# The second down product of a feed-forward, by rounded part for all token tiles first and by low part after

## The reference

```python
h2 = rms_norm(x, norm2_g[l])
x = x + (jax.nn.silu(h2 @ w_ffn_gate[l]) * (h2 @ w_ffn_up[l])) @ w_ffn_down[l]
```

## Time and profile before

| | |
|---|---|
| median of three runs | 2085.47 us |
| the profiled execution | 2088.51 us |
| its span, first to last instruction | 2086.5 us |
| TensorE, VectorE, GpSimd, ScalarE busy | 97%, 65%, 47%, 35% of the span |
| mean granted TensorE clock | 0.993 of full speed |
| one feed-forward chunk | 58.15 us |

### The profile page before, as it was taken

The page is one execution under the profiler, slowest core; times in us unless marked ns, Lnnn a source line. Parts: engine busy times, 40 slices in busy tenths (PEclk is TensorE's granted clock), DMA queues, the critical chain, the costliest instruction groups (busy, mean ns, idle before and its releaser), DMA issues. The chain is left out here.

```text
span 2086.5 us, 30135 instructions
## 1 busy us (share of the span) xinstructions
PE 2021.4 (97%) x9773; PEld 1644.7 (79%) x9773; DVE 1346.1 (65%) x2129; ACT 726.6 (35%) x1294; POOL 977.0 (47%) x827
## 2 busy tenths in 40 slices
PE   6999999999999999999999899997999999999998
PEld 5888888887777777777776788886888888888887
DVE  5768687753467667667657455468667656666666
ACT  4424333311334344334345200016343433333333
POOL 4413232322221122122121243348888889998987
PEclk9999999999999999999999999999999999999999
DMA  4112021223442442342454522210211111101112
GB/s 130 46 31 61 24 57 30 63 69 83 100 102 43 98 98 51 93 108 48 85 133 146 205 91 74 87 61 23 79 61 41 59 60 60 47 33 60 60 60 80
DMA packets 137744, 153.42 MB, mean 74 GB/s; under 512 B 7704, under 2 KB 112160, under 8 KB 137696
## 3 DMA queue, kind: packets, MB, share of 16 engines
q1 hardware_dynamic: 135952, 149.64, 26.1%
q10 hardware_dynamic: 1744, 3.15, 0.4%
HBM read 106.64 MB, written 20.97 MB: 61 GB/s over the span
## 5 line engine op out<-in xcount | busy, mean ns | idle before, releaser
L125 POOL TENSOR_TENSOR w_hi<-w_raw,w_ones 128x64 fp32r<-128x64 f32 x88 | 32.9, 374 | 1005.4 <-PE sb_g L151 463.4
L129 POOL TENSOR_TENSOR w_lo<-w_raw,w_hi 128x512 fp32r<-128x512 f32 x176 | 242.4, 1398 | 7.3
L813 DVE TENSOR_TENSOR sb_wt_lo<-sb_t,sb_wt_hi 128x512 fp32r<-128x512 f32 (+2 forms) x186 | 103.0, 554 | 113.1 <-ACT sb_wt_hi L634 111.3
L151 PE MATMUL sb_g<-h_hi,w_hi 128*128 128x512 f32 x544 | 152.8, 409 | 2.7 <-DVEq L693 1.9
L151 PE MATMUL sb_g<-h_lo,w_hi 128*128 128x512 f32 x544 | 150.5, 401 | 0.0
L151 PE MATMUL sb_g<-h_hi,w_lo 128*128 128x512 f32 x544 | 150.2, 400 | 0.0
L634 ACT CAST sb_wt_hi<-sb_t 128x512 fp32r<-128x512 f32 (+2 forms) x186 | 89.7, 482 | 166.5 <-PE sb_t L500 165.9
L151 PE MATMUL gla_g<-h_hi,w_hi 128*128 128x512 f32 x464 | 124.0, 402 | 0.0
L151 PE MATMUL gla_g<-h_lo,w_hi 128*128 128x512 f32 x464 | 122.8, 397 | 0.0
L151 PE MATMUL gla_g<-h_hi,w_lo 128*128 128x512 f32 x464 | 122.4, 397 | 0.0
L1844 DVE TENSOR_TENSOR y<-mp_out,y 128x512 f32<-128x512 f32 x104 | 70.7, 691 | 67.2 <-PE mp_out L1912 67.2
(11 more groups left out here) (500 smaller groups left out, 5161.5 us busy)
## 6 DMA issues: line engine op xcount, KB each, us to landing
w_raw<-w_in SPq DMA_DIRECT2D x64, 512.0 KB, 8.1
raw_g<-w_ffn_gate SPq DMA_DIRECT2D x11, 1024.0 KB, 5.2
ff_raw_u<-w_ffn_up SPq DMA_DIRECT2D x11, 1024.0 KB, 7.6
ff_raw_d<-w_ffn_down SPq DMA_DIRECT2D x11, 1024.0 KB, 4.8
sb_qs<-sb_q_st SPq DMA_DIRECT2D x32, 256.0 KB, 5.1
sb_kh<-sb_k_st SPq DMA_DIRECT2D x32, 256.0 KB, 5.0
sb_kl<-sb_k_st SPq DMA_DIRECT2D x32, 256.0 KB, 5.0
mp_sig<-gates_t SPq DMA_DIRECT2D x16, 512.0 KB, 4.2
```

The source lines that it names most:

```text
L125: self.nc.gpsimd.tensor_tensor(hi[:, 0:64], raw[:, 0:64], self.ones[:], ALU.mult)
L129: ins = self.nc.gpsimd.tensor_tensor(lo[:, at], raw[:, at], hi[:, at], ALU.subtract)
L151: ins = nc.tensor.matmul(acc, a[:, k, :], b[:, k, half * HALF:(half + 1) * HALF], start=(n == 0), stop=(n == len(steps) - 1))
L813: nc.vector.tensor_tensor(wt_lo[:, m % 2, a:HALF], weight_bank(m, last)[:, a:HALF], wt_hi[:, m % 2, a:HALF], ALU.subtract).then_inc(lo_rea ...
```

## The change

The second down product (P2) first runs hi by hi and hi by lo for the four token tiles, eight matmuls, and then lo by hi for the four, each of which counts its group in d_done. Ahead of the eight it waits for y_high of P2 in place of y_low of P2, and ahead of the last four for y_low. The matmuls of the other six products stay as they were, moved into a small function.

```diff
                 def down_block(ch):
                     for j, p in enumerate(D_ORDER):
                         pe.wait_ge(w_ready, d_first(ch) + j + 1)
-                        if p in (P1, P2, P6, P5):
-                            pe.wait_ge(y_low, 4 * ch + {P1: 1, P2: 2, P6: 3, P5: 4}[p])
+                        if p == P2:
+                            pe.wait_ge(y_high, 7 * ch + Y_HIGH[p])
+                        elif p in (P1, P6, P5):
+                            pe.wait_ge(y_low, 4 * ch + {P1: 1, P6: 3, P5: 4}[p])
                         else:
                             pe.wait_ge(y_low_pool, 3 * ch + {P7: 1, P3: 2, P4: 3}[p])
...
+                        passes = ((y_hi[p], hi), (y_hi[p], lo), (y_lo[p], hi))
+
+                        def multiply_group(g, first, last):
+                            for n in range(first, last):
+                                part, w = passes[n]
+                                ins = nc.tensor.matmul(D_CHAIN[p][g][:], part[:, g * P:(g + 1) * P], w,
+                                                       start=(start and n == 0), stop=(n == 2), skip_group_check=not start)
+                            return ins
+
+                        if p == P2:
+                            for g in range(NG):
+                                multiply_group(g, 0, 2)
+                            pe.wait_ge(y_low, 4 * ch + 2)
+                            for g in range(NG):
+                                multiply_group(g, 2, 3).then_inc(d_done, 1)
+                            continue
                         for g in range(NG):
-                            rows = slice(g * P, (g + 1) * P)
                             if j >= 2:
                                 pe.wait_ge(d_free, d_read(j - 2, g, ch))
-                            passes = ((y_hi[p], hi), (y_hi[p], lo), (y_lo[p], hi))
-                            for n, (part, w) in enumerate(passes):
-                                ins = nc.tensor.matmul(D_CHAIN[p][g][:], part[:, rows], w, start=(start and n == 0),
-                                                       stop=(n == 2), skip_group_check=not start)
-                            ins.then_inc(d_done, 1)
+                            multiply_group(g, 0, 3).then_inc(d_done, 1)
```

## The result

| | before | after |
|---|---|---|
| median of 17 runs each | 2087.66 us | 2091.41 us |
| the profiled execution | 2088.51 us | 2092.41 us |
| its span | 2086.5 us | 2090.4 us |
| one feed-forward chunk, mean of ten | 58.16 us | 58.54 us |

The changed kernel takes 1.0021 times as long, 95% interval 1.0014 to 1.0027: 4.4 us more, between 2.9 and 5.6 (the two medians themselves differ by 3.75). The forecast was 5.3 us more. The two executions differ by 0.7 us before the feed-forward chunks, the changed one being ahead. So times are compared by their distance from the start of the chunk's first down product, in the chunk shown 1537.34 before and 1537.04 after.

The account below looks back on a forecast made before the run. TensorE, busy 97%, was taken as the bound, its largest feed-forward wait before P2. Ten chunks at +0.61 - 0.17 = +0.44 give +4.4, the last +0.9: +5.3 on 2085.47 makes 2090.8 us, range 2081.5 to 2094.

Parts of the forecast that it names:

- P2 starts at once: Second down product: y_hi is ready in time, so it starts without waiting and ends 0.84 us earlier.
- 0.24 a matmul: Bound for P2's matmul spacing when visiting four PSUM tiles twice: 0.16 us a product; 0 was taken.
- VectorE's row then holds TensorE: Down products 2 and 3 wait for VectorE's adds to free PSUM tiles: product 2 by 0.27, product 3 starts 0.51 later.
- the signal: From the end of a recorded instruction to the start on the waiting engine: 0.12 us.
- late weight load: At product 3's start on TensorE: its weight load is not hidden after the wait, costing 0.10 us.
- the third rival: E product keeps its 0.17 and groups 1 to 3 of product 3 wait: +7.9 us, 2093.4 us; chance 12%.
- y_lo of P5 is held for 0.80 us: On VectorE: GpSimd's earlier y_lo of P7 makes it take 1.47 instead of 0.67, delaying every add behind it.
- The loss at E goes: First E product of gate and up: its w_lo is no longer last to come, winning 0.17 us a chunk.
- The last chunk: End of the feed-forward, set by VectorE's row of adds: y_lo of P5 ends later, costing 0.9 us.
- bound for slower: Whole run: a difference counts from 0.2%, 4.2 us, so slower means over 2089.6 us; chance of slower 0.54.
- VectorE wins the turn: Rival at y_lo of P5: GpSimd starts after VectorE, adds not delayed, -0.36 in ten chunks, 2081.9 us; chance 22%.
- The whole wait is won: Rival at P2's wait: 0.84 us won in ten chunks, -8.4 us, 2077.1 us; chance 6%.

Follow-up runs that it names:

- experiment 1: Changed kernel with VectorE's y_lo of P5 one place earlier, ahead of the fourth add of product 0: 2083.07 us, ratio 0.9984 to the kernel before.
- experiment 3: Changed kernel with one more wait, so GpSimd's y_lo of P7 starts only after VectorE's y_lo of P5: 2088.79 us, ratio 1.0009 to the kernel before.
- experiment 4: Changed kernel with one SBUF input of y_lo of P5 replaced by a PSUM tile (wrong number, timing only): 2082.74 us, ratio 0.9980 to the kernel before.
- experiment 7: Changed kernel with GpSimd's sum for P7 moved behind the lo part of the fifth down weights: 2076.61 us, ratio 0.9951 to the kernel before.
- experiment 6: Kernel before, with GpSimd's sum for P7 behind the fifth down weights' lo part and P4's weight sum ahead of y_lo of P7: 2084.13 us, ratio 0.9988.
- experiment 8: Changed kernel with GpSimd's weight sum for P4 moved ahead of y_lo of P7: 2082.89 us, ratio 0.9979 to the kernel before.
- experiment 5: Changed kernel, GpSimd's sum for P7 behind the fifth down weights' lo part, P4's weight sum ahead of y_lo of P7: 2076.6 us, ratio 0.9949 to kernel before.

## Why the prediction was right

The mechanism came out as forecast; two of its terms were mis-sized, in opposite directions, and that the sum still fits within 0.06 us a chunk is partly luck.

- **P2 starts at once.** As forecast: no wait, last matmul 5.21 after the chunk's first (forecast 5.22), nothing for visiting the tiles twice. Shown by the trace after. One bound was misread: the prediction gives 0.24 a matmul "as within P2 before", or 0.16 a product, but the ten matmul steps from 1541.10 to 1543.40 average 0.230, which is the 0.04 that it counts itself elsewhere.
- **VectorE's row then holds TensorE.** P6 0.21 late (forecast 0.27), product 3 at 9.43 (forecast 9.52). Most of the difference is the signal, the first term that was mis-sized: I took 0.12 us, as from y_lo to TensorE. From an add it is 0.05 to 0.06: the add of product 0's first tile ends at 1541.96 + 0.68 = 1542.64 and P6 starts at 1542.69; that of product 1 ends at 1546.41 and product 3 starts at 1546.47.
- **Product 3 is slower than forecast.** The second term: 0.10 was put down for its late weight load, and its 12 matmuls took 2.89 instead of 2.72, 0.17 more. The other 0.07 is of the kind that the third rival names (groups 1 to 3 lose a little); no experiment takes it apart. It offsets the shorter signal.
- **y_lo of P5 is held for 0.80 us.** Measured 1.46 instead of 0.67, 0.79 more; forecast 1.47. That this is the cause, and not a companion, experiments 1, 3 and 4 show, each by another handle: VectorE first, GpSimd later, one input in PSUM. In each y_lo takes 0.68 and product 3 starts 8.63 to 8.85 after the chunk's first product, not 9.43.
- **The loss at E goes.** 2.72 in every chunk instead of 2.83 to 2.92. Counted from the chunk's first product, w_lo of the first E product starts at 34.35 (1571.39 - 1537.04) instead of 34.82, and TensorE arrives later. Experiments 3 and 7 bring the loss back by moving GpSimd's row against TensorE's; experiment 6 takes it away in the kernel before.
- **The sum.** A chunk costs 0.38 more; forecast 0.44. The later start of product 3 is 0.42 and its own pace 0.17, against 0.17 won at E and 0.05 within product 5: 0.37. The last chunk costs 0.8 more from its first product to the last add; forecast 0.9. Ten times 0.38 and 0.8 are 4.6; the runs say 4.4. The forecast time of 2090.8 us lies nearer to the measured 2091.41 than the forecast difference to the measured one. That is luck: it was counted from the median of three runs, 2085.47, and that of 17 is 2087.66. The measured 4.4 also lies barely above the 4.2 that the prediction set as its bound for slower.
- **The rivals.** *VectorE wins the turn* did not happen in the changed kernel, but it describes well what happens once VectorE is not held: forecast 2081.9, that is 0.9983, and experiments 1, 4 and 8 measured 0.9984, 0.9980 and 0.9979. *The whole wait is won* needs VectorE's row freed, as experiment 5 shows: 0.9949, which holds besides the whole wait the loss at E and a shorter end.

What stays open: at what distance exactly a turn is won or lost. In the kernel before, one of VectorE's instructions for the hidden values (line 2447) lost the turn in three chunks, where it came 0.03 or 0.04 ahead of GpSimd's next instruction (1569.18 against 1569.21, and it took 1.87); in the other chunks it came 0.07 to 0.10 ahead and took 0.69. In experiments 5, 6 and 8, y_lo of P5 came 0.04 to 0.07 ahead in all eleven chunks and won each time. So the edge lies near 0.04 us, and the rows, which are given to 0.01, don't place it more closely. The changed kernel's case is clear of it: GpSimd was 0.38 ahead.

## What to carry to other kernels

When a wait on the bound engine goes, ask what its earlier end starts elsewhere, and whether two engines then meet that used to miss each other: here 0.84 us won started GpSimd early enough to hold one VectorE instruction for 0.8 us. Where VectorE and GpSimd both read two SBUF tiles, lay their rows side by side and put the one's waits where the other needs the turn; an instruction moved by one place was worth 7.7 us (1.0021 to 0.9984), and the original idea paid only once VectorE was no longer held.

## What the runs showed of the hardware

- A VectorE tensor_tensor with two SBUF inputs and a GpSimd tensor_tensor exclude each other for whole instructions, in both directions: VectorE 1.46 us instead of 0.68, GpSimd 1.62 to 1.78 instead of 1.29 (the trace after, experiments 1, 5 and 8). With one input in PSUM neither is held (experiment 4: 0.68 and 1.29).
- Of two such instructions that meet while GpSimd has one right behind the other, VectorE's lost the turn when it came 0.03 us ahead of GpSimd's next and took 1.87; it won when it came 0.07 ahead and took 0.68 (experiment 8).
- A signal from VectorE to TensorE took 0.12 us after y_lo and 0.05 to 0.06 us after an add, counted from the recorded end. I had not expected two values, and no run shows why.
- Eight matmuls into four PSUM tiles, two each, and then four that add to the same tiles, start 0.227 us apart, as three in a row to one tile do.
